# Norm statistics of two inputs taken inside the modulation stream, and the key scores and top-16 selections of the expert query taken inside the query product

## Reference, cut to what matters

```python
mod   = silu(c) @ w_ada + b_ada;  mod_c = silu(c_ctx) @ w_ada + b_ada
hc = rmsnorm(ctx, norm1_w) * (1 + csc1) + csh1        # "ctx"
hl = rmsnorm(x,   norm1_w) * (1 + sc1)  + sh1         # "x1"
... = hc @ w_in[:, xbc];  hl @ w_in[:, xbc]           # "xbc", both sides in one product
...
qh = (ht @ w_q).reshape(t, 8, 2, 128)                 # "pq"
sc = einsum('thpd,hpnd->thpn', qh, subkeys)           # key scores
v_top, i_top = top_k(sc, 16)
combo = v_top[:, :, 0, :, None] + v_top[:, :, 1, None, :]
c_val, c_idx = top_k(combo.reshape(t, 8, 256), 16)
gates = softmax(c_val)
out = einsum('tk,tkd->td', gelu(einsum('td,tkd->tk', x, u_tab[i])) * g, v_tab[i])
```

## Time and profile before

| | |
|---|---|
| median of 3 runs | 5165.28 us (5161.29 to 5171.74) |
| profiled execution, its own time | 5184.28 us |
| its span | 5182.5 us |
| busy: PE, DVE, ACT, POOL | 4476.5, 2606.4, 1746.4, 3441.6 us |
| mean granted TensorE clock | 0.916 |

### The profile page before, as it was taken

The page is one execution under the profiler, slowest core; times in us unless marked ns, Lnnn a source line. Parts: engine busy times, 40 slices in busy tenths (PEclk is TensorE's granted clock), DMA queues, the critical chain, the costliest instruction groups (busy, mean ns, idle before and its releaser), DMA issues. The chain is left out here.

```text
span 5182.5 us, 69582 instructions
## 1 busy us (share of the span) xinstructions
PE 4476.5 (86%) x25006; PEld 3731.9 (72%) x25006; DVE 2606.4 (50%) x3829; ACT 1746.4 (34%) x1792; POOL 3441.6 (66%) x1368
## 2 busy tenths in 40 slices
PE   8599645678999996989797999889789999999998
PEld 1489422367888885777586878779678878878877
DVE  0412675735554544231315231139886676676676
ACT  0213343323333333333233333335233333433333
POOL 0238455756888884767385877568478778778776
PEclk9789866789999997999798999999899999999999
DMA  8124343434445543434253444344245445445443
GB/s 315 67 89 179 113 163 129 178 122 146 179 178 186 180 178 116 165 136 162 75 185 129 170 162 170 122 146 155 105 145 180 172 159 181 170 155 183 173 154 130
DMA packets 111034, 803.77 MB, mean 155 GB/s; under 512 B 12903, under 2 KB 13192, under 8 KB 14088
## 3 DMA queue, kind: packets, MB, share of 16 engines
q1 hardware_dynamic: 108720, 787.30, 42.2%
q10 hardware_dynamic: 2200, 14.90, 0.8%
HBM read 800.06 MB, written 2.10 MB: 155 GB/s over the span
## 5 line engine op out<-in xcount | busy, mean ns | idle before, releaser
L374 POOL TENSOR_TENSOR w_lo<-ring,w_hi 128x1024 fp32r<-128x1024 f32 x1304 | 3156.1, 2424 | 1504.4 <-ACT w_hi L936 1504.1
L936 ACT ACTIVATE w_hi<-ring 128x1024 fp32r<-128x1024 f32 x1304 | 1377.0, 1060 | 2440.1 <-PE psum L415 2052.7
L413 PE MATMUL psum<-hc_hl,w_hi 128*128 128x512 f32 x5568 | 1996.3, 402 | 105.5 <-DVE hc_hl L1234 43.4
L415 PE MATMUL psum<-hc_hl,w_lo 128*128 128x256 f32 x5568 | 1569.5, 282 | 0.0
L413 PEld LDWEIGHTS psum<-hc_hl,w_hi 128*128 128x128 f32 x5568 | 1056.2, 190 | 367.8 <-issue 65.9
L415 PEld LDWEIGHTS psum<-hc_hl,w_lo 128*128 128x128 f32 x5568 | 1062.2, 191 | 0.1
L413 PE MATMUL psum<-out_hl,w_hi 128*128 128x512 f32 x2048 | 740.8, 406 | 46.4 <-DVE out_hl L1914 32.2
L415 PE MATMUL psum<-out_hl,w_lo 128*128 128x256 f32 x2048 | 581.9, 284 | 0.0
L413 PEld LDWEIGHTS psum<-out_hl,w_hi 128*128 128x128 f32 x2048 | 391.1, 191 | 154.5 <-DVE out_hl L1914 38.5
L415 PEld LDWEIGHTS psum<-out_hl,w_lo 128*128 128x128 f32 x2048 | 395.0, 193 | 0.0
L413 PE MATMUL psum<-hid_hl,w_hi 128*128 128x512 f32 x1024 | 366.2, 401 | 14.0 <-DVE hid_hl L1626 14.0
(11 more groups left out here) (355 smaller groups left out, 5177.2 us busy)
## 6 DMA issues: line engine op xcount, KB each, us to landing
ring<-stream SPq DMA_DIRECT2D x748, 1024.0 KB, 4.8
x<-x ACTq DMA_DIRECT2D x2, 2048.0 KB, 11.0
ctx_raw<-ctx ACTq DMA_DIRECT2D x1, 2048.0 KB, 9.4
mem_raw<-mem ACTq DMA_DIRECT2D x1, 2048.0 KB, 7.7
out<-x SPq DMA_DIRECT2D x4, 512.0 KB, 2.7
filt_w<-filt_w ACTq DMA_DIRECT2D x1, 1024.0 KB
dft<-dft ACTq DMA_DIRECT2D x1, 1024.0 KB
window<-window ACTq DMA_DIRECT2D x1, 1024.0 KB, 12.3
```

The costliest lines, as they stand in the source:

```text
L374: pool.tensor_tensor(w_lo[:, slot], ring[:, s, k], w_hi[:, slot].bitcast(F32), ALU.subtract).then_inc(lo_ready, 1)
L413: pe.matmul(psum[:, b, :].rearrange("p (s t) -> p s t", s=2), w_hi[:, slot, c], x_hl, start=start(c), stop=False, skip_group_check=True)
L415: m = pe.matmul(psum[:, b, 0:T], w_lo[:, slot, c], x_hl[:, 0], start=False, stop=stop(c), skip_group_check=True)
L936: act.activation(w_hi[:, 2 * (s % 2) + h], ring[:, s, k], ACT.Copy).then_inc(hi_ready, 1)
```

## The change

1. The squares, sums and roots of `ctx` and `x` are taken between the groups of the modulation: DVE sums the squares after group 1 (`ctx`) and group 3 (`x`), PE's `norm_pe` stands behind groups 3 and 5, and `to_unit` multiplies the whole of `ctx_raw` and `x` by the reciprocal root in place. After `scales` there remains, per four chunks and side, a scaling with bias on DVE, the same with rounding on ACT, and a subtraction. Both sides alternate by four chunks, and PE may start "xbc" after the first four chunks of each.
2. Inside "pq", after tile n, PE makes the key scores of tile n-1 for both halves of the tokens, ACT copies them (256 columns), and DVE picks the 16 best of half head n-1 and, after each second, the best sums of the head. The gates' tables of both token halves follow after the stage.
3. ACT splits the first two up tiles within its "pq" loop, and EARLY is 16: 16 up tiles without gates, then 16 with 2 gate groups each.

```diff
-EARLY = 24
+EARLY = 16
@@ PE
+        for i in range(ADA_G):
...
+            if i == 3:
+                norm_pe("ctx")
+            if i == 5:
+                norm_pe("x1")
...
-        norm_pe("ctx")
-        norm_pe("x1")
-        pe.wait_ge(norm_lo, 8)
...
+                        if j == 0 and k % 4 == 0:
+                            pe.wait_ge(norm_lo, 2 * (k // 4) + 2)
...
-        linear("pq", h_hl, after="ffn")
-        pe.wait_ge(bank_free, 4 + bank_of["peer"])
-        for tb in range(2):
-            for k in range(16):
-                m = pe.matmul(psum[:, 4 * tb + k // 4, (k % 4) * P:(k % 4) * P + P], q_peer[:, k, tb * P:tb * P + P],
-        pe.wait_ge(p_scc, 2)
+        def key_scores(k):
+            pe.wait_ge(bank_free, 4 + bank_of["pq"] + k + 1)
+            if k >= 4:
+                pe.wait_ge(p_scc, k - 3)
+            for tb in range(2):
+                m = pe.matmul(psum[:, 4 + k % 4, tb * P:tb * P + P], q_peer[:, k, tb * P:tb * P + P],
+                              subkeys[:, k], start=True, stop=True)
             m.then_inc(p_sc, 1)
...
+        for n in range(KC):
+            pe.wait_ge(bank_free, bank_of["pq"] + n + 1)
+            for h in range(2):
+                half_wide(FIRST["pq"] + n, n % RING, h, lambda c: h == 0 and c == 0,
...
+                key_scores(n - 1)
+        key_scores(KC - 1)
@@ ACT
-        act.wait_ge(s_mod, 1)
-        norm_act("ctx", ctx_raw, lambda k: mod[:, k, 1:2])
-        act.wait_ge(norm_lo, 4 * NS["ctx"] + 4)
-        norm_act("x1", x, lambda k: mod[:, k, 0:1], ahead=FIRST["xbc"])
+        norm_act("ctx", ctx_raw, split=False)
+        act.wait_ge(norm_half, 2)
+        norm_act("x1", x, split=False)
+        split_tile(FIRST["xbc"], FIRST["xbc"] // RING, 0)
+        split_tile(FIRST["xbc"] + 1, FIRST["xbc"] // RING, 1)
+        act.wait_ge(s_scales, 2)
+        act.wait_ge(plain_done, 2)
+        for q in range(4):
+            for src, hi, side in ((ctx_raw, c_hi, 1), (x, h_hi, 0)):
+                for k in range(4 * q, 4 * q + 4):
+                    m = act.activation(hi[:, k], src[:, k], ACT.Identity, scale=scales[:, side, k:k + 1],
+                                       bias=mod[:, k, side:side + 1])
+                m.then_inc(norm_hi, 1)
...
+        for n in range(2, KC + 2):
+            g = FIRST["pq"] + n
+            split_tile(g, g // RING, g % RING)
+            if n >= 3:
+                scores_out(n - 3)
+        scores_out(KC - 1)
@@ DVE
+        def to_unit(name, src):
...
+            st.did(dve.reciprocal(nrstd[:], nrt[:]))
+            st.settle()
+            dve.tensor_tensor(src[:], src[:], nrstd[:].unsqueeze(1).broadcast_to([P, KC, T]),
+                              ALU.mult).then_inc(plain_done, 1)
...
+            if i == 1:
+                norm_half_sum("ctx", 0)
+                norm_half_sum("ctx", 1)
+            if i == 3:
+                to_unit("ctx", ctx_raw)
+                norm_half_sum("x1", 0)
+                norm_half_sum("x1", 1)
+            if i == 5:
+                to_unit("x1", x)
...
+        for n in range(KC):
+            dve.wait_ge(half_done, 2 * (FIRST["pq"] + n) + 2)
+            both(q_peer[:, n], n % RING).then_inc(bank_free, 1)
+            if n >= 1:
+                best_of_half(n - 1)
+            if n >= 2 and n % 2 == 0:
+                best_of_head(n // 2 - 1)
+        best_of_half(KC - 1)
+        best_of_head(PEER_H - 1)
```

More of the change, by code:

```diff
@@ L445, in _ @@
         pe.wait_ge(acc_free, 4)
[L446 to L456, removed]
+        for i in range(ADA_G):
+            pe.wait_ge(ada_copied, i + 1)
+            for j in range(RING):
+                pe.wait_ge(landed[j], 16 * i + 16)
+                wide = ring[:, j].rearrange("p k n -> p (k n)")
+                for k in range(4):
+                    m = pe.matmul(psum[0:2, 4 + i % 2, :], c_silu[:, 4 * j + k], wide[:, 512 * k:512 * k + 512],
+                                  start=j + k == 0, stop=j + k == 6)
+                    if k % 2:
+                        m.then_inc(half_done, 1)
+            if i == 3:
+                norm_pe("ctx")
+            if i == 5:
+                norm_pe("x1")
         pe.wait_ge(ada_copied, 2 + ADA_G)
@@ L1085, in _ @@
         act.dma_start(ret_decay[:], a["ret_decay"]).then_inc(s_aux[3], 16)
-        norm_act("mix", x, ready=lambda q: (plain_done, q + 1), ahead=FIRST["ret"])
+        norm_act("mix", x, ready=lambda q: (plain_done, 2 + q + 1), ahead=FIRST["ret"])
         act.dma_start(pos_i[:], a["pos"]).then_inc(s_aux[4], 16)
@@ L1147, in _, with scores_out @@
         norm_act("ffn", x, ready=lambda q: (bank_free, 4 + bank_of["o"] + 4 * (q + 1)), ahead=FIRST["pq"])
[L1148 to L1151, removed]
+        def scores_out(k):
+            act.wait_ge(p_sc, k + 1)
+            act.activation(psc[:, :, k], psum[:, 4 + k % 4, 0:T].rearrange("p (b n) -> p b n", b=2),
                            ACT.Copy).then_inc(p_scc, 1)
+        for n in range(2, KC + 2):
[4 more added lines that the diff above has]
+        scores_out(KC - 1)
         def up_act(q, first, tiles):
@@ L1798, in _, with top16 @@
         norm_dve("ffn", x, lambda k: col("ffn", k), summed=1)
-        copy_stage("pq", q_peer)
         LEAST = -3.0e38
[L1803 to L1809, removed]
-                st.settle()
-                for k in range(rows):
-                    st.did(dve.max_index(index[:, k, e], best[:, k, e], src[:, k]))
-                for k in range(rows if r == 0 else 0):
-                    st.did(dve.match_replace(spare[:, k], best[:, k, e], values[:, k], LEAST))
+        def top16(values, spare, best, index):
+            st.settle()
+            for tb in range(2):
+                st.did(dve.max(best[:, tb, 0:8], values[:, tb]))
+            st.settle()
+            for tb in range(2):
+                st.did(dve.match_replace(spare[:, tb], best[:, tb, 0:8], values[:, tb], LEAST))
+            for tb in range(2):
+                st.did(dve.max_index(index[:, tb, 0:8], best[:, tb, 0:8], values[:, tb]))
+            st.settle()
+            for tb in range(2):
+                st.did(dve.max(best[:, tb, 8:16], spare[:, tb]))
+            st.settle()
+            for tb in range(2):
+                st.did(dve.max_index(index[:, tb, 8:16], best[:, tb, 8:16], spare[:, tb]))
@@ new lines, in _, with best_of_half, best_of_head @@
+        combo = psc[:].rearrange("p b (h x) n -> p b h (x n)", x=2)
+        spare1 = psc2[:, 0:2]
+        spare2 = psc2[:, 2:6].rearrange("p (b x) n -> p b (x n)", x=2)
+        def best_of_half(k):
+            dve.wait_ge(p_scc, k + 1)
+            top16(psc[:, :, k], spare1, top_v[:, :, k], top_u[:, :, k])
+        def best_of_head(h):
+            st.settle()
+            to = [P, TOPK, TOPK]
+            for tb in range(2):
+                st.did(dve.tensor_tensor(combo[:, tb, h].rearrange("p (x y) -> p x y", x=TOPK),
+                                         top_v[:, tb, 2 * h].unsqueeze(2).broadcast_to(to),
+                                         top_v[:, tb, 2 * h + 1].unsqueeze(1).broadcast_to(to), ALU.add))
+            top16(combo[:, :, h], spare2, com_v[:, :, h], com_u[:, :, h])
```

97 lines of the change are left out of this document (54 added, 43 removed).

## The result

The changed kernel takes **5093.83 us** (median of 4 runs, 5088.97 to 5100.25) against 5163.28 (median of 4, 5160.32 to 5171.74): ratio 0.9866, 95% interval 0.9853 to 0.9879, that is 69.5 us less (62 to 76). The forecast was 90 less. The profiled execution is the slowest of the four (5100.25 us), and that of before (5184.28) lay above each of its timed runs; so their spans differ by 84 us, and I read differences stage by stage, from one trace of each kernel.

The account below looks back on a forecast made before the run. PE was busy 4476.5 of 5182.5 us, so a change pays only where PE waits. Gains of 44.5 + 2 + 43.6 = 90 us took 5184.3 to 5094, the median 5165.3 to 5075; range 5058 to 5105.

Parts of the forecast that it names:

- the first rival: In "pq", DVE falls behind by two POOL instructions a head; stage ends at 131.4, not 105.5; 5101 us; chance 0.17.
- head: Start to first "xbc" tile: norms move into "ada", tile done at 166 instead of 210.5; gain 44.5 us, 40 to 47.
- "pq" and start of the up tiles: Query product with selections inside, ending 105.5 us after its start, then first up tiles; gain 2 us, -24 to 6.
- eight early tiles less: Before the exponential: EARLY from 24 to 16 takes 8 tiles of 5.83 us, 46.6 us, out of the stretch.
- gate groups: 32 groups after the early tiles: PE sets the pace at 3.24 us each, 103 us against 100.3; costs 3 us.
- the third: In "pq", MATCH_REPLACE8 and FIND_INDEX8 wait for POOL, 2.1 us each, 285 us in the stage; 5360 us; chance 0.04.
- the warm start of the up tiles: After "pq", up tiles no longer begin cold: two tiles take 11.6 us instead of 15.0; credited 3.4 us.
- the second rival: Gate groups in lock-step: PE and DVE wait by turns, 3.55 us per group, 10 us lost; 5085 us; chance 0.11.
- the quarter's gain: Expert quarter: 46.6 us from fewer early tiles less 3 in the gate groups; gain 43.6 us, bounds 33 and 47.
- Slack of the exponential: After "pq": DVE has about 61 us of work left while PE takes 93 for 16 tiles; slack 30 us.

Follow-up runs that it names:

- the head alone: Kernel before with only the norm statistics moved into the modulation stream (modulation loop, norms, scales, later counts): 5126.08 us, ratio 0.9926.

## Why the forecast came out as it did

The kernel got faster by the parts that the forecast named, and by 69.5 us where it had 90. The measured 5093.83 lies in the stated range of 5058 to 5105, but outside the 5062 to 5090 that the forecast gave itself: the part of the range that holds it stood there for the first rival, which didn't occur. So the range held in part by luck. Side by side, in us gained, by the traces of before and after:

| term | forecast | measured | how |
|---|---|---|---|
| head | 44.5 (40 to 47) | 44.3 | 210.53 less 166.20 |
| "pq" and start of the up tiles | 2 | -0.7 | 109.1 less 109.8 |
| eight early tiles less | 46.6 | 42.8 | 150.7 less 107.9 |
| gate groups | -3 | -8.2 | 119.3 less 127.5, to the first down sum |
| down tiles | 0 | -2.7 | 185.0 less 187.7 |
| sum | 90 | 75.5 | |

**The head was right in each step**: four scalings with two column operands took 1.38 us where I took 1.4, the subtraction 0.419 where I took 0.426, a step 2.84 for 2.9, TensorE ended the tile 5.0 us after the last chunk, and the later stages gave nothing back that a run can tell (the head alone: 565.7 in the stretches for 564.1, 38 us in the time with 44 inside its interval).

**"pq" was right in kind**: two tiles took 12.65 us (3402.36 to 3415.00), VectorE's pace, where I had 13.0, and in each head but the last one of the two pair sums waited for POOL, 2.2 us in the first head and some 0.9 in the six others, which is the 0.9 that I had taken. So two POOL instructions a head, the first rival, have fallen, and the third with them: MATCH_REPLACE8 stayed at 275 to 278 ns. The term was off by 2.7 in the sum around it. I credited the warm start of the up tiles with 3.4 us, and it gave 1.4: from the first up product to the second GELU 15.05 us before (3510.66 to 3525.71), 13.66 now (3467.11 to 3480.77). TensorE had waited 5.88 us for VectorE's last copy just ahead of it, and the stage took 0.7 longer than my 105.5.

**The step that failed is "so 8 tiles of 5.83 us, 46.6, leave the stretch", not by the price of a tile but by what it put at nothing**: that the tables cost the tiles that stay as much as before. A tile that moves is worth 5.76 us, as the run with 24 early tiles shows. But beside the tables the changed kernel loses 5.9 us, which came back with their scratch in PSUM, and the kernel before lost some 2.5 (128.18 for 22 tiles, where 79.67 for 14 undisturbed ones and 46.0 for eight more make 125.7). That is 3.5 of the 3.8 missed. TensorE's waits for POOL from 3300 to 3850 us point the same way, in the kernel before:

```profile
PE psum L402 <- POOL w_lo L374: 7.9, 4, 5.4
```

Less the 5.4 at the first up tile that is 2.5 us, against 4.7 of the 6.0 in the changed kernel (the waits from 3476 to 3567). The table instructions are the same (the kernel before has two wide pair sums besides). Before, they came in two runs, one per token half, from 3543.3 to 3566.0 and from 3607.9 to 3630.6, with selections between; now they form one, from 3478.3 to 3528.2. That POOL, which works up to four half tiles ahead of TensorE, could make up for more of two short runs than of one long run fits these times, but no run splits the tables to show it. I had named the port as a matter of additions in "pq" and not asked it of the instructions eight times as wide, 20 us later.

**Gate groups**: TensorE sets the pace, as forecast, and the second rival (3.55 a group, in lock-step) has fallen, though the quarter's gain of 34.6 (42.8 less 8.2) came near the 33 that I had kept for it. The term was mis-sized by 5 us in three places. A group takes 3.286 us (3593.93 to 3685.96 over 28) where I had 3.24 and the kernel before 3.19: 3.0 us over 31, half of it forecast. At the end VectorE waits 2.32 us for the last group of a TensorE that it had been ahead of before. And 2.8 us lie between the first `hid` (82.4 us earlier) and the first down sum (79.6 earlier): POOL's four back-to-back halves met three instructions of the first block before (1.69 us, 2.31 and 2.44) and meet four of the first two blocks now. With the product in PSUM 2.1 of it are gone. One reading of rows was off and cancels in the sum: 3674.62 is the second one-hot, the first started at 3672.05, so the way from the last GELU to it was 18.2 us (17.9 now) and not 20.7, and that to the first `hid` 102.9 and not 100.3.

**Slack of the exponential**: 40.3 us, 30 forecast; VectorE's own 61 us of work behind the stage were right (3467.1, the first up product, to 3528.2), TensorE was later.

**Open.** Down tiles of the first quarter take 187.3 to 187.8 us in four kernels and 184.0 to 185.0 in seven, with the same work; one with 24 early tiles has 186.9. All four kernels that move the exponential, and that with the product in PSUM, have the lower value, so it may go with how the stage starts, but no run isolates it. And 75.5 by the traces stands against 69.5 by the medians (62 to 76): the same instructions from the first "xbc" tile to the first `q_peer` copy took 3201.8 us in the profiled run of before and 3195.9, 3200.4, 3187.0 and 3187.4 in four others, and behind the second quarter's start, where the two kernels do the same, the trace of before is another 7 us longer (1206.1 us for 1199.0). What makes that spread isn't settled.

## What to carry to other kernels

When a change shortens a stream of tiles that has another engine's work beside it, price two things: the tiles that go, and what that work costs the tiles that stay, in its new order. In a shared-port pair ask it of the widest instructions first, and of both sides. A wait in the queue of an engine that also feeds others (ScalarE's exponential ahead of the splits) costs what is queued behind it: issue the next inputs first, then wait. And where a trace shows an engine waiting 40 us for another, ask first what could be moved ahead of that wait.

## What the hardware showed

A VectorE scaling of 256 elements took 352 ns with one column operand and one operation, 407 with two of each. MAX8, FIND_INDEX8 and MATCH_REPLACE8 never waited for POOL, which was busy 77 of 107 us beside them (on 128 elements 274 to 296, 283 to 290 and 275 to 278 ns; MATCH_REPLACE8 on 256 elements 407 to 410). POOL is held as well as holding: 3.46 us a half tile in place of 2.40 beside wide VectorE instructions with two SBUF inputs. The same instructions over 3.2 ms took 3187.0 to 3201.8 us in five executions.
